# Decoder layer on one core: the Mamba time steps move into the samples' attention, and the first three stream units run in plain fp32

## The chip, the cores and the metric

One core of a Trainium2 chip runs the whole layer as one launch. The metric is the device time of that launch in microseconds (us), lower is better. The reference's inputs and outputs are fp32.

## What is computed

One decoder layer for a prompt of 1024 tokens and 8 samples of one token each, 1032 tokens in all, width 1024. Cut to what the change touches:

```python
mod = (silu(c) @ w_ada + b_ada)          # 9 rows (prompt, 8 samples), 6 parts: sh1 sc1 g1 sh2 sc2 g2
h = rmsnorm(x, norm1_g) * (1 + sc1) + sh1
z, xs, bm, cm, dtr, q, k, v, qi, ki, wi, gs, ga = split(h @ w_in)
dt = softplus(dtr + dt_bias); A = -exp(a_log)      # 32 heads
Acs = cumsum(dt * A)   # in each of 8 chunks of 128 tokens
decay_end = exp(Acs[-1] - Acs); chunk_decay = exp(Acs[-1]); exp(Acs)
y_attn = attend(q, k, v, qi, ki, wi)     # samples: pages of the cache, 64 of 257 keys kept
x = x + g1 * (merged @ w_out); h2 = rmsnorm(x, norm2_g) * (1 + sc2) + sh2; x = x + g2 * ffn(h2)
```

## The kernel before

The layer is a row of stages, each a block in which the five engines have instruction streams of their own, joined by semaphores; between two blocks all engines meet at a barrier. In order: `first_norm`, `project`, `select`, `attend` (prompt), `attend_samples`, `steps`, `stream`, `scan`, `merge`, `project_out_and_norm`, `ffn`. The token buffer `hT` holds h as 128 partitions x 8 x 1032, in fp32. A plain fp32 product is one matmul per 128 of the 1024 inputs, 8 for a unit of 128 outputs x 344 tokens. A split product writes each factor as a rounded half and a rest (`_hi`, `_lo`, fp32r) and takes three matmuls in place of one (`product`, L2253 to L2255), 24 for a unit.

**`attend_samples`** (L971). SP, ACT and POOL read the page table and issue page loads: SP first stores `qT` of the prompt (L1019, 4 MB), then 6 index-key pages and all 16 value pages; ACT 10 index-key pages; POOL all 16 key pages (L1008). TensorE (PE) turns the samples' small rows (L1034 to L1041), the index pages (L1048), makes the scores (L1056, L1059), turns the key pages (L1067), adds up mask and logits (L1071, L1075), turns the probabilities (L1080) and multiplies by the value pages (L1088). VectorE (DVE) finds the 64th score (L1144 to L1158), does the softmax (L1160 to L1166) and writes the result into `qT` (L1176); SP stores it (L1024), and the block ends when that has landed.

**`steps`** (L1180) stands between it and `stream`. SP loads a 0/1 table of heads, the modulation sums (`s_mod`, four partial sums over row groups) and its bias (L1209 to L1211). DVE makes dt by a chain of some 20 dependent instructions on 128 x 264 (L1302 to L1326), while ACT rounds `hT` (`s_h_hi`, L1228) and DVE then takes the rests (`s_h_lo`, L1330, written over `hT`). PE adds up the modulation (L1255), the decays (L1272 to L1274), spreads head values over partitions (L1279) and makes four gate tiles (L1263), which ACT copies and SP stores (L1217). POOL adds the bias (L1246) and splits the first two weight slabs for `stream` (L1352, L1354).

**`stream`** (L1361) makes the rest of the input projection in 102 units (34 blocks of 128 outputs x 3 token thirds), first 12 units of group 0's z, then for each further group 18 units of x/B/C and 12 of z. Unit u goes to PSUM bank u % 4 and waits until ACT has taken unit u-4 out of it (`keep_z` L1614, `keep_x` L1626). A weight slab of 256 outputs serves six units; POOL splits slab j+1 when unit 6j is free to overwrite the other half of `s_w_hi`/`s_w_lo`. Beside the units, DVE splits the cumulated decays (L1765, L1767) and makes the causal convolutions of group 0, six blocks f of five instructions each (L1679 a copy of the tail, L1680, three of L1683; `convolve`), then the samples' part; ACT's order is written out: the SiLU of block f (L1601) stands behind the copies of units 3, 4, 6, 8, 9 and 11 and waits for convolution f. After unit 11 PE turns the six tails (`raw_rows`, L1554, L1560), and after units 14 and 18 it spreads the samples' B and C, which POOL has laid out (L1507, L1571).

## Time and profile before

| | |
|---|---|
| median of 3 runs | 2978.61 us (2975.07 to 2980.99) |
| profiled execution, its own time | 2978.76 us |
| its span | 2977.0 us |
| PE busy | 2754.8 us, 93% of the span |
| DVE / ACT / POOL busy | 52% / 23% / 27% |
| mean clock granted to PE | 0.954 of full |

PE is the engine that bounds most of the span; the slices in which its digit falls below 9 are where another engine or a DMA decides. The granted clock has two levels, 1.2 and 2.4 GHz, 0.5 and 1.0 in the rows.

### The profile page before, as it was taken

The page shows a single profiled execution, that of the slowest core. Times are in us where ns is not written, and L with a number is a line of the kernel's source. Part 1 is how long each engine was busy: PE and PEld are TensorE (multiplying, and loading weights), DVE is VectorE, ACT ScalarE, POOL GpSimd, SP SyncE. Part 2 cuts the span into 40 slices and gives each one's busy share as a digit, 9 for nine tenths or more (in the row PEclk, how much of TensorE's full clock was granted, in tenths as well). Part 3 has the DMA queues.
Part 4 walks back from the last instruction along what each step waited for, and adds up shares of the span by engine and source line. Part 5 has one row for each costly group of instructions (what it writes and reads, how often), then busy time and mean ns, then how long its engine had stood idle before and what let it go on. Part 6 is the DMA issues. An engine that isn't in the chain of part 4 may idle for free. (4 is left out here: it accounts for less than half of the span.)

```text
span 2977.0 us, 40645 instructions
## 1 busy us (share of the span) xinstructions
PE 2754.8 (93%) x16375; PEld 2343.0 (79%) x16375; DVE 1546.4 (52%) x2733; ACT 680.7 (23%) x1432; POOL 812.0 (27%) x486
## 2 busy tenths in 40 slices
PE   7999999998996678999979979998979999999997
PEld 4888556666785368999956669998878989898986
DVE  3313399904553357665659963554634242525155
ACT  3121211105774211221247741101210000000001
POOL 0000430004321124434326642231242222232220
PEclk9999999997998679999989989999989999999999
DMA  6110234520002144434156644333111111111111
GB/s 219 46 58 22 68 121 151 170 71 11 2 2 101 54 138 145 136 107 143 58 141 197 184 139 140 114 100 107 29 44 49 51 43 43 43 43 45 55 29 57
DMA packets 288663, 258.63 MB, mean 87 GB/s; under 512 B 21273, under 2 KB 265361, under 8 KB 288290
## 3 DMA queue, kind: packets, MB, share of 16 engines
q1 hardware_dynamic: 254780, 190.35, 21.4%
q10 hardware_dynamic: 26176, 56.16, 5.2%
q0 software_dynamic: 7520, 9.51, 1.0%
q8 instruction: 131, 2.15, 0.3%
q14 instruction: 56, 0.46, 0.1%
HBM read 191.04 MB, written 65.06 MB: 86 GB/s over the span
## 5 line engine op out<-in xcount | busy, mean ns | idle before, releaser
L2253 PE MATMUL ps<-h_lo,w_hi 128*128 128x344 f32 x1504 | 482.5, 321 | 18.0 <-DVE h_lo L2372 11.1
L2254 PE MATMUL ps<-h_hi,w_hi 128*128 128x344 f32 x1504 | 481.4, 320 | 0.0
L2255 PE MATMUL ps<-h_hi,w_lo 128*128 128x344 f32 x1504 | 481.3, 320 | 0.0
L2235 POOL CAST w_hi<-ring 128x2048 fp32r<-128x2048 f32 (+1 forms) x50 | 96.4, 1928 | 813.5 <-PE ps L2255 785.5
L2253 PEld LDWEIGHTS ps<-h_lo,w_hi 128*128 128x128 f32 x1504 | 284.1, 189 | 19.1 <-issue 18.4
L2255 PEld LDWEIGHTS ps<-h_hi,w_lo 128*128 128x128 f32 x1504 | 283.9, 189 | 0.0
L2254 PEld LDWEIGHTS ps<-h_hi,w_hi 128*128 128x128 f32 x1504 | 283.6, 189 | 0.2
L2253 PE MATMUL ps<-s_h_lo,s_w_hi 128*128 128x344 f32 x816 | 265.4, 325 | 0.0
L2254 PE MATMUL ps<-s_h_hi,s_w_hi 128*128 128x344 f32 x816 | 260.8, 320 | 0.0
L2255 PE MATMUL ps<-s_h_hi,s_w_lo 128*128 128x344 f32 x816 | 260.8, 320 | 0.0
L467 PE MATMUL ps<-ring,hT 128*128 128x256 f32 (+3 forms) x1152 | 237.8, 369 | 5.9 <-PEq L119 5.9
L2691 DVE TENSOR_TENSOR ps<-ps,f_silu 128x344 f32<-128x344 f32 x66 | 34.6, 525 | 392.9 <-ACT f_silu L2657 392.9
L2237 POOL TENSOR_TENSOR w_lo<-ring,w_hi 128x2048 fp32r<-128x2048 f32 (+1 forms) x50 | 234.2, 4683 | 4.0
L467 PEld LDWEIGHTS ps<-ring,hT 128*128 128x128 f32 (+1 forms) x1152 | 197.2, 182 | 43.9 <-issue 8.7
L618 PE MATMUL ps<-hT,ring 128*128 128x344 f32 x768 | 227.2, 455 | 0.0
L618 PEld LDWEIGHTS ps<-hT,ring 128*128 128x128 f32 x768 | 144.3, 190 | 80.9 <-ACT sig L653 5.4
L2657 ACT ACTIVATE f_silu<-ps 128x344 f32<-128x344 f32 x66 | 30.3, 458 | 719.7 <-PE ps L2255 719.7
L681 DVE TENSOR_SCALAR_CACHE_REDUCE reached<-score,threshold_bits 128x384 uint8<-128x384 f32 (+5 forms) x192 | 171.5, 943 | 35.7 <-POOL score L574 33.4
L888 DVE CUSTOM_DVE_ANT_0 prob<-ps,sel_bias 128x128 f32<-128x128 f32 (+7 forms) x128 | 96.9, 757 | 155.7 <-PE ps L819 154.7
L2253 PE MATMUL ps<-w_lo,a_hi 128*128 128x512 f32 (+1 forms) x396 | 157.2, 397 | 8.5 <-DVE f_scaled L2704 8.4
L2253 PEld LDWEIGHTS ps<-s_h_lo,s_w_hi 128*128 128x128 f32 x816 | 153.7, 188 | 2.6 <-issue 2.6
L2255 PE MATMUL ps<-w_hi,a_lo 128*128 128x512 f32 (+1 forms) x396 | 155.8, 393 | 0.0
(415 smaller groups left out, 5229.6 us busy)
## 6 DMA issues: line engine op xcount, KB each, us to landing
ring<-in_w_ada SPq DMA_DIRECT2D x24, 1024.0 KB, 7.5
ring<-in_w_in SPq DMA_DIRECT2D x23, 1024.0 KB, 5.7
ring<-in_w_ffn_in SPq DMA_DIRECT2D x44, 512.0 KB, 4.8
ring<-in_w_in SPq DMA_DIRECT2D x24, 512.0 KB, 8.4
s_post<-post ACTq DMA_DIRECT2D x24, 512.0 KB, 2.6
post_chunk<-s_post SPq DMA_DIRECT2D x32, 384.0 KB, 3.7
ring<-in_w_ffn_out SPq DMA_DIRECT2D x10, 1024.0 KB, 5.1
s_sig<-sig ACTq DMA_DIRECT2D x16, 516.0 KB, 6.9
```

Source lines behind the costliest of these rows:

```text
L467: mm = nc.tensor.matmul(ps[0:r, (9 * s + t) % 4, 0:width], hT[:, k, P * t:P * t + r], w[:, k, 0:width], start=(k == 0), stop=(k == KB - 1))
L618: mm = nc.tensor.matmul(ps[:, j % 4, 0:CW], w[:, k, 0:P], hT[:, k, CW * c:CW * c + CW], start=(k == 0), stop=(k == KB - 1))
L681: a = v.tensor_scalar(reached[:, at:at + P * (i + 1)], score_of(i), thr_f[:, i:i + 1], None, ALU.is_ge, ALU.add, accum_out=count[:, i:i + 1])
L888: nc.vector.tensor_tensor_reduce(out=prob[:, n % 2, 0:L], in0=ps[:, 2 * (n % 2):2 * (n % 2) + 2, :].rearrange("p a n -> p (a n)")[:, chunk ...
L2235: self.nc.gpsimd.tensor_copy(hi, raw).then_inc(self.hi_done, 1)
L2237: self.nc.gpsimd.tensor_tensor(lo, raw, hi.bitcast(F32), ALU.subtract).then_inc(self.split, 1)
L2253: nc.tensor.matmul(out, ah, bl, start=(i == 0), stop=False)
L2254: nc.tensor.matmul(out, ah, bh, start=False, stop=False)
L2255: mm = nc.tensor.matmul(out, al, bh, start=False, stop=(i == len(terms) - 1))
L2657: nc.scalar.activation(silu[:, i % 2, :], ps[:, 2 * (i % 3), 0:CW], ACT.Silu).then_inc(silu_done, 1)
L2691: v.tensor_tensor(prod, prod, silu[:, i % 2, :], ALU.mult).then_inc(act_done, 1)
```

## The change

The block `steps` is gone. Its chain for dt, the decays, the modulation, the head spread and the gates are worked out inside `attend_samples`, in gaps of each engine's stream. The bias of the modulation is no longer added by POOL: it is loaded into rows 16 to 24 of the same tile, and a 0/1 matrix `pick` adds it up with the partial sums. The gates are kept as 9 rows and spread over 128 partitions when they are loaded later. Key and value pages share one buffer, so a value page is loaded when its sample's key pages have been turned. The loads are placed anew on the three queues. The rounding of `hT` and the taking of its rests move into `stream`, on ACT and DVE; the first three units (the first block, three token thirds) are made from `hT` and the unsplit slab in plain fp32, and a third's rest is written over `hT` when its plain unit is done. POOL splits slabs 0 and 1 inside `stream`. The diff, cut (the parts of `steps` that come back word for word in `attend_samples` stand there once):

```diff
@@ attend_samples @@
-def attend_samples(K, T):
+def attend_samples(K, T, S):
...
-        kpage, vpage = sb("kpage", [P, DEC, NPAGE, 256]), sb("vpage", [P, DEC, NPAGE, 256])
+        kpage = vpage = sb("kv_page", [P, DEC, NPAGE, 256])
...
         @block.gpsimd
         def _(pool):
             pool.wait_ge(table_in, 16)
-            load_pages(pool, "cache_k", kpage, k_in, 0, 16)
+            load_pages(pool, "cache_k", kpage, k_in, 0, 8)
 
         @block.sync
         def _(sp):
             sp.dma_start(pages[:], A["page_table"].rearrange("b j -> (b j)").unsqueeze(0)).then_inc(table_in, 16)
             sp.dma_start(who[:], A["k_who"]).then_inc(who_in, 16)
+            sp.wait_ge(table_in, 16)
+            load_pages(sp, "cache_kidx", ipage, i_in, 0, 8)
+            load_pages(sp, "cache_k", kpage, k2_in, 8, 16)
             sp.dma_start(A["s_att"].rearrange("k p n -> p k n")[:, :, 0:SEQ], T.qT[:, :, 0:SEQ]).then_inc(y_out, 16)
-            sp.wait_ge(table_in, 16)
-            load_pages(sp, "cache_kidx", ipage, i_in, 0, 6)
-            load_pages(sp, "cache_v", vpage, v_in, 0, 16)
+            for b in range(DEC):
+                sp.wait_ge(pe_key, b + 1)
+                load_pages(sp, "cache_v", vpage, v_in, NPAGE * b, NPAGE * b + NPAGE)
+            for i in range(2):
+                sp.wait_ge(gate_done, i + 1)
+                sp.dma_start(A["s_gates"][i], mod[0:9, 3 * D * i:3 * D * i + D]).then_inc(gate_out, 16)
             sp.wait_ge(y_done, 1)
             sp.dma_start(A["s_att"].rearrange("k p n -> p k n")[:, :, SEQ:NT], T.qT[:, :, SEQ:NT]).then_inc(y_out, 16)
             sp.wait_ge(y_out, 32)
+            sp.wait_ge(gate_out, 32)
...
-            pe.wait_ge(step, 1)
+            pe.wait_ge(step, 4)
...
-            pe.wait_ge(k_in, 16 * DEC * NPAGE)
+            pe.wait_ge(k_in, 16 * 8)
+            pe.wait_ge(k2_in, 16 * 8)
...
+            pe.wait_ge(dta_done, 1)
+            dta = S.dta[:].rearrange("p c h -> p (c h)")
+            mm(ps[:, 0, 0:NC], K.le[:], dta, start=True, stop=True)
+            mm(ps[:, 0, NC:2 * NC], K.gt[:], dta, start=True, stop=True)
+            mm(ps[:, 1, 0:NC], K.ones[:], dta, start=True, stop=True).then_inc(sums, 1)
+            pe.wait_ge(mod_in, 48)
+            pe.wait_ge(pick_done, 5)
+            for a, part in enumerate((1, 2)):
+                for k in range(KB):
+                    m = mm(ps[:, 2, (8 * a + k) * 9:(8 * a + k) * 9 + 9], mod[:, D * part + P * k:D * part + P * k + P], pick[:],
+                           start=True, stop=True)
+            m.then_inc(modT_ps, 1)
...
+            pe.wait_ge(sdec, 1)
+            pe.wait_ge(modT_step, 1)
+            pe.wait_ge(head_in, 16)
+            for b in range(INNER // P):
+                m = mm(ps[:, 2, 144 + 17 * b:144 + 17 * b + 17], mod[0:HEADS, D + P * b:D + P * b + P], spread[:],
+                       start=True, stop=True)
+            m.then_inc(spread_ps, 1)
...
+            pe.wait_ge(decays, 3)
+            for i, bank in enumerate((0, 4)):
+                for h in range(2):
+                    m = mm(ps[0:9, bank + h, :], pick[:], mod[:, 3 * D * i + 512 * h:3 * D * i + 512 * h + 512],
+                           start=True, stop=True)
+                m.then_inc(gate_ps, 1)
...
+            nc.scalar.activation(a_row[:], K.heads_row[:, 1, :], ACT.Exp).then_inc(a_done, 1)
+            nc.scalar.activation(a_col[:], K.heads_col[:, 1:2], ACT.Exp).then_inc(a_done, 1)
+            act.wait_ge(arg_ready, 1)
+            nc.scalar.activation(e[:], e[:], ACT.Exp).then_inc(dt_exp, 1)
             act.wait_ge(table_in, 16)
-            load_pages(act, "cache_kidx", ipage, i_in, 6, 16)
+            load_pages(act, "cache_kidx", ipage, i_in, 8, 16)
+            for rows in (slice(0, 16), slice(25, P)):
+                act.dma_start(mod[rows, :], A["s_mod"][rows, :]).then_inc(mod_in, 16)
+            act.dma_start(mod[16:25, :], A["b_ada"][0, 2 * D:6 * D].partition_broadcast(9)).then_inc(mod_in, 16)
...
+            act.wait_ge(modT_ps, 1)
+            act.dma_start(mod[0:HEADS, D:3 * D], A["k_head"]).then_inc(head_in, 16)
+            act.wait_ge(sdec_arg, 1)
+            nc.scalar.activation(spread[:, 0:DEC], spread[:, 0:DEC], ACT.Exp).then_inc(sdec, 1)
+            act.wait_ge(sums, 1)
+            for src, dst in ((ps[:, 0, 0:NC], S.e_acs), (ps[:, 0, NC:2 * NC], S.d_end), (ps[:, 1, 0:NC], S.c_dec)):
+                nc.scalar.activation(dst[:].rearrange("p c h -> p (c h)"), src, ACT.Exp).then_inc(decays, 1)
...
+            for i, bank in enumerate((0, 4)):
+                act.wait_ge(gate_ps, i + 1)
+                nc.scalar.copy(mod[0:9, 3 * D * i:3 * D * i + D], ps[0:9, bank:bank + 2, :].rearrange("p a n -> p (a n)"))\
+                    .then_inc(gate_done, 1)
...
+            link(v.memset(u[:, NC:W], 0.0))
+            link(v.tensor_tensor(u[:, 0:NC].rearrange("p (c h) -> p c h", h=HEADS), K.dt_raw[:],
+                                 K.heads_row[:, 0, :].unsqueeze(1).to_broadcast([P, TT, HEADS]), ALU.add))
+            link(v.tensor_scalar(u[0:HEADS, NC:W], K.dtT_raw[:], K.heads_col[:, 0:1], None, ALU.add))
+            v.scalar_tensor_tensor(e[:], u[:], -1.0, u[:], ALU.mult, ALU.min).then_inc(arg_ready, 1)
...
+            dve.wait_ge(dt_exp, 1)
+            link(v.tensor_scalar(t[:], e[:], 2.0, None, ALU.add))
...
+            v.tensor_scalar(spread[:, 0:DEC], u[0:HEADS, NC:W], a_col[:], None, ALU.mult).then_inc(sdec_arg, 1)
+            v.scalar_tensor_tensor(S.which[:], K.ident[:, 0:GH], -1.0, K.ident[:, GH:2 * GH], ALU.mult, ALU.subtract)
+            v.tensor_copy(pick[:], K.ident[:, 0:9]).then_inc(pick_done, 1)
+            for q, c0 in enumerate((16, 32, 64, 96)):
+                dve.wait_ge(pick_done, q + 1)
+                v.tensor_tensor(pick[:], pick[:], K.ident[:, c0:c0 + 9], ALU.add).then_inc(pick_done, 1)
...
+            dve.wait_ge(modT_ps, 1)
+            v.tensor_copy(K.modT[:, 2:4].rearrange("p a k s -> p (a k s)"), ps[:, 2, 0:144]).then_inc(modT_step, 1)
...
+            dve.wait_ge(spread_ps, 1)
+            v.tensor_copy(S.hx[:].rearrange("p b s -> p (b s)"), ps[:, 2, 144:144 + 17 * 16])
@@ steps @@
-def steps(K, S):
...
@@ stream @@
-def stream(K, S):
+def stream(K, hT, S):
+    PLAIN = TC
...
                             sp.wait_ge(K.sw_split, j + 1)
+                            if j == 0:
+                                sp.wait_ge(gemm, PLAIN)
...
             v.memset(pre[:, :, 0:CONV - 1], 0.0).then_inc(conv_zeroed, 1)
+            split_stream_slab(K, S, pool, 0)
...
-                if 2 <= j + 1 < NSLAB:
+                if j + 1 < NSLAB:
...
-                    pe.wait_ge(K.sw_split, i // 2 + 1)
+                    pe.wait_ge(*(ring_landed(K, first) if u < PLAIN else (K.sw_split, i // 2 + 1)))
+                elif u == PLAIN:
+                    pe.wait_ge(K.sw_split, 1)
+                if PLAIN <= u < 2 * PLAIN:
+                    pe.wait_ge(h_split, u - PLAIN + 1)
...
+                if u < PLAIN:
+                    for k in range(KB):
+                        a = mm(ps[:, u % 4, 0:CW], slab_of(K, first)[:, k, w], hT[:, k, cols], start=(k == 0), stop=(k == KB - 1))
+                    a.then_inc(gemm, 1)
+                    return
...
+            for c in range(TC):
+                cols = slice(CW * c, CW * c + CW)
+                a.copy(h_hi[:, :, cols], hT[:, :, cols]).then_inc(h_rounded, 1)
...
+            for c in range(TC):
+                cols = slice(CW * c, CW * c + CW)
+                dve.wait_ge(h_rounded, c + 1)
+                dve.wait_ge(gemm, c + 1)
+                v.tensor_tensor(h_lo[:, :, cols], hT[:, :, cols], h_hi[:, :, cols].bitcast(F32), ALU.subtract).then_inc(h_split, 1)
@@ project_out_and_norm @@
-                sp.dma_start(gate[0:r, b, :], A["s_gates"][b, 0:r, :]).then_inc(gate_in, 16)
+                sp.dma_start(gate[0:r, b, :], A["s_gates"][0, 0].partition_broadcast(P) if b == 0 else A["s_gates"][0, 1:9, :]).then_inc(gate_in, 16)
@@ program @@
-    A["s_gates"] = nc.dram_tensor("s_gates", (4, P, D), F32, kind="Internal").ap()
+    A["s_gates"] = nc.dram_tensor("s_gates", (2, 9, D), F32, kind="Internal").ap()
...
+        with ExitStack() as place:
+            h_lo = place.enter_context(nc.sbuf_tensor("s_h_lo", [P, KB, NT], F32R, side="right"))
```

How the written order moves: PE in the samples' attention, from the last key page on (names: `kpage`/`kv_page` cache pages, `sbias` the mask, `mod` the modulation sums, `spread` the head values). Before:

```order
L1067 MATMUL ps<-ident,kpage 128x128 x3
L1071 MATMUL ps<-sbias,who 128x257 [waits sbias_done,skT_done]
L1075 MATMUL ps<-skT,sqx 128x257 x16
L1080 MATMUL ps<-ident,sprob 128x128 [waits sdiag_done]
L1080 MATMUL ps<-ident,sprob 128x128
L1081 MATMUL ps<-sdiag,whoT 8x128
L1085 MATMUL ps<-snew,v 128x128 [waits value_pages_in,spT_done]
```

Now, with the changed kernel's line numbers:

```order
L1095 MATMUL ps<-s_dta,le 128x256 [waits dta_done]
L1096 MATMUL ps<-s_dta,gt 128x256
L1097 MATMUL ps<-s_dta,ones 128x256
L1102 MATMUL ps<-mod_pick,mod 128x9 [waits mod_pick_done,mod3_in]
L1102 MATMUL ps<-mod_pick,mod 128x9 x15
L1107 MATMUL ps<-sbias,who 128x257 [waits sbias_done,skT_done]
L1111 MATMUL ps<-skT,sqx 128x257 x16
L1118 MATMUL ps<-spread,mod 128x17 [waits head_in,modT3_step,sdecay_done]
L1118 MATMUL ps<-spread,mod 128x17 x15
L1123 MATMUL ps<-ident,sprob 128x128 [waits sdiag_done]
```

19 matmuls stand ahead of the mask's and 16 more behind the logits; four more (L1137, the gates) end PE's stream.

POOL at the start of the stream (names: `s_w_hi`/`s_w_lo` a slab's halves, `segw` a table for the scan). Before:

```order
L1490 MEMSET pre 128x4x3
L1491 CAST segw<-ones 128x4096
L1494 DMA s_acs<-acs_rows 32x2x1024 [waits n1turned]
```

Now:

```order
L1437 MEMSET pre 128x4x3
L1295 CAST s_w_hi<-ring 128x2048 [waits slab_landed0]
L1297 TENSOR_TENSOR s_w_lo<-ring,s_w_hi 128x2048 [waits stream_w_rounded]
L1439 CAST segw<-ones 128x4096
L1442 DMA s_acs<-acs_rows 32x2x1024 [waits n1high_moved]
L1446 DMA segw<-s_acs 8x4x1024 [waits n1low_moved,acs_stored]
L1446 DMA segw<-s_acs 8x4x1024
L1295 CAST s_w_hi<-ring 128x2048 [waits slab_landed1]
L1297 TENSOR_TENSOR s_w_lo<-ring,s_w_hi 128x2048 [waits stream_w_rounded]
```

Two slab splits now stand in this block, one ahead of the cast of `segw` and one behind its loads. On DVE, at the same place:

```order
L1725 CAST acs_rows<-ps 32x1024 [waits n1sample_step]
L1727 TENSOR_TENSOR acs_rows<-ps,acs_rows 32x1024 [waits n1high_moved]
L1732 TENSOR_TENSOR s_h_lo<-hT,s_h_hi 128x8x344 [waits modT_step,n1mean] x3
L1639 COPY tail<-pre 128x11 [waits mod_product,n1turned]
L1640 TENSOR_SCALAR post<-pre,vecs 128x1024
```

The three subtractions that make the rests stand ahead of all six convolutions of group 0; before, the first convolution followed the split of the decays. (Semaphores are lent again under the name of an earlier owner, as `n1mean` here.)

## Rows read from the trace of the kernel before

**Rows 1.** Busy time by stretch: the samples' attention, then `steps`.

```profile
core 0: us, PE busy (x) PEld busy (x) DVE busy (x) ACT busy (x) POOL busy (x), PEclk, DMA share, GB/s
944.00:1026.50 82.50, 49.95 (x203) 32.36 (x203) 17.87 (x61) 10.61 (x22) 8.70 (x17) 0.63 0.33 109
1026.50:1086.50 60.00, 28.23 (x86) 18.52 (x87) 40.37 (x37) 12.82 (x15) 22.36 (x8) 0.59 0.17 61
```

**Rows 2.** Timeline, samples' loads: start us, us, engine, line [idle before <-releaser].

```profile
946.34 15.23 ACTq L1008 DMA_DIRECT2D ipage<-in_cache_kidx  x10
...
957.00 17.51 SPq L1008 DMA_DIRECT2D vpage<-in_cache_v  x16
...
964.87 3.60 PE L1048 MATMUL ps<-ident,ipage 128*64 128x128 f32 x16 [17.22 <-DMA ipage<-in_cache_kidx]
```

**Rows 3.** DMA issues of 940 to 1100 us: KB each, us to landing.

```profile
s_att<-qT SPq DMA_DIRECT2D x1, 4096.0 KB, 15.4
```

**Rows 4.** Timeline, the two gaps of PE at the mask and the softmax.

```profile
993.21 1.19 PE L1071 MATMUL ps<-sbias,who 8*128 8x257 f32 x2 [4.77 <-DVE sbias L1158]
...
1006.55 0.44 PE L1080 MATMUL ps<-ident,sprob 128*128 128x128 f32 x2 [2.71 <-DVE sdiag L1166]
```

**Rows 5.** Groups by line in `steps`: busy us, mean ns | idle before.

```profile
L1330 DVE TENSOR_TENSOR s_h_lo<-hT,s_h_hi 128x2752 fp32r<-128x2752 f32 x3 | 8.9, 3005 | 0.0
...
L1255 PE MATMUL ps<-mod_who,mod 128*128 128x9 f32 x32 | 7.0, 363 | 19.3 <-POOL mod L1246 19.3
L1279 PE MATMUL ps<-spread,head_x 32*128 32x17 f32 x32 | 7.0, 370 | 7.0 <-DVE modT L1333 7.0
...
L1238 ACT COPY gate_sb<-ps 8x1024 f32<-8x1024 f32 x2 | 2.0, 1000 | 0.8 <-PE ps L1263 0.8
...
L1272 PE MATMUL ps<-s_dta,le 128*128 128x256 f32 x2 | 1.2, 712 | 2.9 <-DVE s_dta L1322 2.9
```

**Rows 6.** Timeline, the end of the samples' attention, and the gates in `steps`.

```profile
1022.40 1.47 DVE L1176 COPY qT<-ps 64x16 f32<-64x16 f32 x8 [14.45 <-PE ps L1088]
1023.90 0.38 SPq L1024 DMA_DIRECT2D s_att<-qT  x1
1026.48 0.35 SPq L1209 DMA_DIRECT2D head_x<-in_k_head  x1
...
1048.54 6.25 PE L1263 MATMUL ps<-mod,mod_who 128*128 128x512 f32 x8
```

**Rows 7.** Plain and split units: a group of the page, and where 12 split units start and end.

```profile
L618 PE MATMUL ps<-hT,ring 128*128 128x344 f32 x768 | 227.2, 455 | 0.0
...
1090.05 0.66 PE L2253 MATMUL ps<-s_h_lo,s_w_hi 128*128 128x344 f32 x1
...
1136.07 0.55 PE L1554 MATMUL ps<-ident,small_rows 24*128 24x24 f32 x6
```

**Rows 8.** Timeline of DVE and POOL in the stream: convolutions 0 and 3, slab split.

```profile
1092.54 0.15 DVE L1679 COPY tail<-pre 128x11 f32<-128x11 f32 x1
...
1093.45 3.93 DVE L1683 SCALAR_TENSOR_TENSOR post<-pre,vecs,post 128x1024 f32<-128x1024 f32 x3
...
1113.54 1.91 POOL L1352 CAST s_w_hi<-ring 128x2048 fp32r<-128x2048 f32 x1 [12.80 <-PE ps L2255]
...
1113.90 1.57 DVE L1679 COPY tail<-pre 128x11 f32<-128x11 f32 x1 [7.01 <-DMA s_post<-post]
...
1115.53 5.12 POOL L1354 TENSOR_TENSOR s_w_lo<-ring,s_w_hi 128x2048 fp32r<-128x2048 f32 x1
...
1116.22 8.17 DVE L1683 SCALAR_TENSOR_TENSOR post<-pre,vecs,post 128x1024 f32<-128x1024 f32 x3
```

**Rows 9.** PE's one long wait in the stream, and the stretch behind it (columns of rows 1).

```profile
1173.28 3.57 PE L1571 MATMUL ps<-bc_diag,ones 128*128 128x512 f32 x4 [7.76 <-POOL bc_diag L1507]
...
1173.00:1177.00 4.00, 3.72 (x6) 1.82 (x7) 0.00 (x0) 0.87 (x2) 4.00 (x5) 0.56 0.53 203
```

**Rows 10.** A stretch within the logits: us, PE busy, clock, DMA share, GB/s.

```profile
1000.00:1004.00 4.00, 3.84 (x18) 1.00 0.00 0
```

More of the change, by code:

```diff
@@ L753, in _ @@
             sp.dma_start(own_head[:], A["k_head"][0:AH, 0:D]).then_inc(head_in, 16)
+            for s in K.finished:
+                sp.sem_clear(s)
         @block.gpsimd
@@ L991, in attend_samples @@
         stat = sb("sstat", [P, 4])
+        NC = TT * HEADS
+        W = NC + DEC
+        u, e, z, t, poly = (sb("dt_" + n, [P, W]) for n in "uezts")
+        a_row, a_col = sb("a_row", [P, HEADS]), sb("a_col", [HEADS, 1])
+        spread = sb("spread", [HEADS, 17])
+        mod = sb("mod3", [P, 4 * D])
+        pick = sb("mod_pick", [P, 9])
+        pick_done = K.sem("mod_pick_done")
+        mod_in, modT_ps, modT_step = K.sem("mod3_in"), K.sem("modT3_in_psum"), K.sem("modT3_step")
+        gate_ps, gate_done, gate_out = K.sem("gate_in_psum"), K.sem("gate_done"), K.sem("gate_stored")
+        arg_ready, dt_exp, a_done = K.sem("dt_arg"), K.sem("dt_exp"), K.sem("a_exp")
+        dta_done, sums, decays = K.sem("dta_done"), K.sem("decay_sums"), K.sem("decays_done")
+        sdec_arg, sdec, spread_ps = K.sem("sdecay_arg"), K.sem("sdecay_done"), K.sem("spread_in_psum")
+        k2_in, head_in = K.sem("more_key_pages_in"), K.sem("head_in")
         table_in, who_in = K.sem("page_table_in"), K.sem("who_in")
@@ L1158, in _ @@
             v.tensor_scalar(sbias[:], swk[:], -OFF, None, ALU.mult).then_inc(biased, 1)
+            dve.wait_ge(modT_ps, 1)
+            v.tensor_copy(K.modT[:, 2:4].rearrange("p a k s -> p (a k s)"), ps[:, 2, 0:144]).then_inc(modT_step, 1)
+            dve.wait_ge(modT_step, 1)
+            sc = K.modT[:, 3, :, :]
+            v.tensor_scalar(sc, sc, 1.0, None, ALU.add).then_inc(modT_step, 1)
+            dve.wait_ge(modT_step, 2)
+            v.tensor_tensor(sc, sc, K.vecs[:, 128:136].unsqueeze(2).to_broadcast([P, KB, 9]), ALU.mult)
             dve.wait_ge(pe_logit, 1)
@@ L2796, in program, with kept_right @@
-            K.finished, K.lent = K.lent, []
             with ExitStack() as rec:
                 S = Chip()
-                S.dt, S.dta, S.d_end, S.e_acs, S.c_dec = (sb("s_" + n, [P, TT, HEADS], rec) for n in ("dt", "dta", "end", "e", "c"))
-                S.hx = sb("s_hx", [P, INNER // P, 17], rec)
-                S.which = sb("which_head", [P, GH], rec)
-                S.ysT = K.ysT
-                mid.close()
+                with ExitStack() as att:
+                    K.finished, K.lent = K.lent, []
+                    T = Chip()
+                    T.qT = sb("qT", [P, KB, NT], att)
+                    T.v = sb("v", [P, TT + 1, KVH * HD], att)
+                    T.wi = sb("wi", [P, TT + 1, IH], att)
+                    T.q_s, T.k_s = sb("q_s", [DEC, D], att), sb("k_s", [DEC, KVH * HD], att)
+                    T.qi_s, T.ki_s = sb("qi_s", [DEC, IH * HD], att), sb("ki_s", [DEC, HD], att)
+                    T.dt_raw, T.dtT_raw = K.dt_raw, K.dtT_raw
+                    with ExitStack() as keys:
+                        T.kT = sb("kT", [P, KVH, SEQ], keys)
+                        T.bias = keys.enter_context(nc.sbuf_tensor("sel_bias", [P, BIAS_AT[TT]], BF16))
+                        with ExitStack() as index:
+                            T.kiT, T.qiT = sb("kiT", [P, SEQ], index), sb("qiT", [P, 2, SEQ], index)
+                            with ExitStack() as rope:
+                                K.cos, K.sin = (sb(n, [P, TT + 1, HD], rope) for n in ("cos", "sin"))
+                                project(K, hT, T)
+                                release(K.finished)
+                            select(K, hT, T)
+                        K.finished, K.lent = K.lent, []
+                        attend(K, T)
+                        release(K.finished)
+                    def kept_right(name, shape):
+                        return rec.enter_context(nc.sbuf_tensor(name, shape, F32, side="right"))
+                    S.dt, S.dta, S.d_end, S.e_acs, S.c_dec = (kept_right("s_" + n, [P, TT, HEADS]) for n in ("dt", "dta", "end", "e", "c"))
+                    S.hx, S.which = kept_right("s_hx", [P, INNER // P, 17]), kept_right("which_head", [P, GH])
+                    S.ysT, S.h_lo = K.ysT, h_lo
+                    attend_samples(K, T, S)
@@ L2804, in program @@
+                K.finished, K.lent = K.lent, []
+                S.segw = rec.enter_context(nc.sbuf_tensor("segw", [P, GROUPS, TT, P], F32R))
                 with ExitStack() as parts:
-                    S.h_lo, S.h_hi = (parts.enter_context(nc.sbuf_tensor(n, [P, KB, NT], F32R, side="right")) for n in ("s_h_lo", "s_h_hi"))
+                    S.h_hi = parts.enter_context(nc.sbuf_tensor("s_h_hi", [P, KB, NT], F32R, side="right"))
                     S.w_hi, S.w_lo = (parts.enter_context(nc.sbuf_tensor(n, [P, 2, SLAB], F32R, side="right")) for n in ("s_w_hi", "s_w_lo"))
-                    steps(K, S)
@@ L2808, in program @@
-                    release(K.finished)
-                    S.segw = rec.enter_context(nc.sbuf_tensor("segw", [P, GROUPS, TT, P], F32R))
-                    K.finished, K.lent = K.lent, []
-                    stream(K, S)
+                    stream(K, hT, S)
                 release(K.finished)
                 K.finished, K.lent = K.lent, []
-                merged = mid.enter_context(nc.sbuf_tensor("merged", [P, KB, NT], F32, side="right"))
-                scan(K, S, W, merged)
+                scan(K, S, W, hT)
```

194 lines of the change are left out of this document (21 added, 173 removed).

## The prediction

> **What bounds the kernel now.** I read the page first: PE is busy for 93% of the span, so time is won only where PE idles or runs at the half clock. The busy time by stretch shows such a place [rows 1]: the samples' attention and `steps` together hold 142.5 us in which PE works 50.0 of 82.5 and 28.2 of 60.0 us, at a mean clock of 0.63 and 0.59. In `steps` no engine fills the time: DVE has 40.4 us, POOL 22.4, PE 28.2. PE's first matmul there waits 19.3 us for POOL's bias addition, which waited for a load, and its head spread 7.0 us for DVE [rows 5]. In the samples' attention the timeline shows PE's gaps: 17.2 us until the index pages are there [rows 2], 4.8 us for the mask and 2.7 us for the softmax, both from DVE [rows 4]. The stream behind is the opposite: 12 units follow each other from 1090.05 to 1136.07 us without a gap [rows 7].
>
> **The change, term by term,** against the profiled execution, which took 2978.76 us itself (span 2977.0; the median is 2978.61, so no correction is needed).
>
> *`steps` goes*: from its first instruction at 1026.48 us [rows 6] to the start of the stream at 1086.5 [rows 1]: **-60.0 us**, its barrier included.
>
> *Loads of the samples*: ACT issued 10 index pages in 15.2 us, 1.52 each, while the 4 MB store that SP had issued first was moving for 15.4 us; behind that store SP issued 16 value pages in 17.5 us, 1.09 each [rows 2, 3]. PE started 3.3 us after ACT's last issue (961.6 to 964.9). Now 8 pages each are issued on SP and ACT ahead of the store. At 1.09 each they end at 946.3 + 8.7 = 955.1, and PE starts at 958.4: **-6.5 us**. If the pace stays 1.52, it is -3.0. Key pages follow on SP (8 more, until some 964) and are turned only after the scores. The last keys were turned at 993.21 - 4.77 = 988.4 [rows 4], now at 982; even if all 16 value pages were issued only then, 17.5 us later makes 999.5, and they are needed behind the softmax, at 1006.55 + 3.4 = 1010 by the terms below. DVE's dt chain goes into its wait for the scores; it costs nothing while it is shorter than that wait. In `steps` those small instructions took long only beside POOL's additions, and POOL adds nothing here.
>
> *PE ahead of the mask*: three sums of some 1.1 to 1.2 us (one of their rows stands) and 32 passes in 7.0 us for the modulation [rows 5], 10.4 us, of which 4.8 fit in the gap [rows 4]: **+5.6 us**. All these durations come from half-clock stretches; at the full clock the work would be 5.2 us and the term +0.4.
>
> *Head spread behind the logits*: 7.0 us [rows 5] against a gap of 2.7 [rows 4]: **+4.3 us**, at the full clock +0.8.
>
> *Gates at the end*: eight passes as in L1263, 6.25 us; a copy by ACT of 1.0 [rows 5, 6]; an issue of 0.4; then the issue and landing of the last store as now, 1026.48 - 1023.90 = 2.6. With 0.2 for handovers that makes 10.5 us behind PE's value products, where it was 1026.48 - 1022.40 = 4.1 [rows 6]: **+6.4 us**, with the passes at the full clock +3.3.
>
> *Plain units*: 768 passes of L618 are 48 plain units in 227.2 us, 4.73 each; a split unit takes 46.02 / 12 = 3.84 [rows 7]. Three: **+2.7 us**.
>
> *DVE's late start*: counted from the stream's start. Before, convolution 0 began at +6.0 (1092.54). Now the third rest waits for plain unit 2, which ends at 4.1 + 14.2 = +18.3, and takes 3.0 [rows 5]: DVE begins at +21.3, 15 us later. And it meets POOL there. DVE's tail copy took 1.57 us in place of 0.15, ending with POOL's cast, and three of L1683 took 8.17 in place of 3.93 while POOL's subtraction ran [rows 8]: the two engines take turns, whole instruction by whole instruction. POOL splits slab 0 and casts `segw` until about +10, waits some 7 for its store, splits slab 1 from about +19 and slab 2 from +29.4, the end of unit 5. With turns taken in that order the first convolution ends at +39 in place of +10.7, the next ones follow at 4.8 us each, and the sixth tail is read at about +59. Who waits: ACT's SiLU of block 0 stands ahead of its copy of unit 4, whose bank unit 8 needs (due at +36.9, starts at +40.6: 3.7 us; then 1.0 at unit 9); `raw_rows` comes at +56.9 and waits 2.9 for the sixth tail; the first spread behind unit 14 waits 1.6, since the samples' convolution follows DVE's backlog. Together 9.2 us. PE's existing wait of 7.8 us for POOL [rows 9] gets 1.7 shorter by this, as POOL is less behind: **+7.5 us**. The bounds are 0 (DVE and POOL never meet) and 11.
>
> The Trainium skill, page "SBUF — State Buffer", section "Who interferes with whom", has the loser of the shared port pair wait for the whole instruction, as rows 8 show, but lets a DVE instruction with one SBUF input run free; by that the split of the decays would not queue behind POOL, and this term would be about 0.8 us less.
>
> *Hidden*: POOL's splits are due at +21.8 (slab 0) and +29.4 (slab 1) and end near +7 and +28; if slab 1 is later, unit 6 waits one for one. ACT's three roundings lie beside the plain units, and the first is asked for at +8. The later gate loads move the same bytes ahead of a stage that PE fills.
>
> Sum: -60.0 - 6.5 + 5.6 + 4.3 + 6.4 + 2.7 + 7.5 = -40.0 us: **2939 us**.
>
> **Rivals.**
>
> *A. The samples' part is cheaper* (the added passes at the full clock). For it: the logits ran at clock 1.0 from 1000 to 1004 us [rows 10], and PE now has work in its gaps. Against it: the mean is 0.63 there, and the same passes left it at a mean of 0.59 in `steps` [rows 1]. The four terms become -6.5 + 0.4 + 0.8 + 3.3 = -2.0 in place of +9.8: 2927 us.
>
> *B. DVE's lag costs PE nothing* (four banks and a SiLU order with slack). For it: DVE idled 7.0 us ahead of convolution 3 [rows 8], so there was slack. Against it: the lag is 15 us before POOL is counted. Only +2.7 is left in the stream: 2931 us.
>
> *C. The new waits cost PE its clock.* PE's wait of 7.8 us was followed by a stretch at 0.56, in which four matmuls took 3.57 us; at the full clock these would be 3.57 x 0.56 = 2.0, so 1.6 us lost and some more in the unit behind, about 2 [rows 9]. Three waits of 2.9, 3.7 and 1.6 us would add up to 6: 2945 us. Against it: they are shorter than that one. The Trainium skill, page "TensorE: Matmul & The Clock Gate", section "Part 1: The HAM clock gate", lets the array fall back to the half clock after idling, which speaks for this rival; that a short idle is enough no row here shows.
>
> *D. The modulation load is late.* 2 MB more go through ACT's queue beside 2 MB of keys and the 4 MB store. At the store's pace (4 MB in 15.4 us) [rows 3] all of it takes some 31 us from 946, thus until 977, and PE asks at about 985. Eight us are in reserve; if the queues serve the load last and it lands at 995, PE waits 10 us: 2949 us.
>
> *E. Slower than before.* If the half clock of rows 9 doesn't end with one wait but holds through the z units of group 0 and beyond, because PE meets DVE's backlog at each bank, every unit costs 3.8 us more. The gain of 40 is gone after 10.5 of the 102 units; with 12 it is 2985 us. Against it: the 12 units of rows 7 began after 10 us without dense work and still average 3.84 us, so the clock comes back once units follow each other. That `steps` is not really removed is excluded: its instructions are absent from the written order.
>
> **How the numbers follow.** Sum as worked out 0.45, A 0.17, B 0.15, C 0.10, D 0.08, E 0.02; 0.03 for something I don't see, half of it slower. The forecast is the likeliest case. The range reaches to A (2927) and to D (2949) with the bounds of the terms beyond (A with a free stream is 2919, the longer lag 2943): 2924 to 2951 leaves out less than 2 in 10. A measurement of this kernel can tell 0.2%, 6 us, from no change; no case but E comes near that: faster 0.96, same 0.01, slower 0.03.
>
> **What would show it.** Index pages turned at about 958 us; the block of the samples ending near 1036, 91 to 93 us after its start in place of 82; in the stream two waits of PE on ACT near units 8 and 9, one on DVE's tails behind unit 11; three plain units of 4.7 us. Wrong it would be if PE waited in the samples' part for the modulation or the head table, if unit 5 waited for the third rest, or if units 3 to 8 took more than 3.9 us each.

## The result, and the profile after

| | before | changed |
|---|---|---|
| median, 20 runs of each, alternating | 2978.39 us (2973.71 to 2982.04) | 2982.47 us (2977.51 to 2987.88) |
| profiled execution, its own time | 2978.76 us | 2977.51 us |
| its span | 2977.0 us | 2975.7 us |
| PE busy, mean clock | 93%, 0.954 | 92%, 0.956 |

The ratio of the times is 1.0015, with a 95% interval of 1.0009 to 1.0021: the changed kernel is slower by some 4 us, less than the 0.2% that the prediction had taken for no change. The prediction was 2939 us, 2924 to 2951. It was wrong by 43 us. The profiled execution of the changed kernel is the lowest of its 20, 5 us under their median, so its trace is read for where time lies, and the medians say how much.

Four stretches divide the span: up to the first load of the samples' attention, that block (with `steps` where it is there), `stream` up to the first row store behind its last group, and the rest.

| stretch, us | before | forecast | changed | difference |
|---|---|---|---|---|
| up to the samples' attention | 944.1 | 944.1 | 942.5 | -1.6 |
| samples' attention (+ `steps`) | 142.4 | 92.2 | 135.6 | -6.8 |
| `stream`, up to that store | 386.4 | 396.6 | 397.8 | +11.4 |
| the rest | 1504.1 | 1504.1 | 1499.8 | -4.3 |

The stream cost what was forecast. The block did not: 43 us of the expected 50 are missing there. Its windows, as in [rows 1] (in the second fence PE alone is counted):

```profile
core 0: us, PE busy (x) PEld busy (x) DVE busy (x) ACT busy (x) POOL busy (x), PEclk, DMA share, GB/s
942.50:1078.00 135.50, 70.89 (x281) 46.38 (x281) 29.14 (x96) 14.25 (x31) 4.40 (x8) 0.58 0.27 85
```

```profile
core 0: us, PE busy (x), PEclk, DMA share, GB/s
984.00:994.00 10.00, 10.00 (x23) 0.50 0.06 26
994.00:1004.00 10.00, 2.73 (x6) 0.50 0.06 26
```

PE has 70.9 us of work and 64.6 us of nothing. The second fence shows what it waits for: from 984 to 1004 us the DMA engines are busy for 0.06 of their time, which is one of 16, and move 26 GB/s. The DMA issues of the block give the load (KB each, us to landing):

```profile
s_att<-qT SPq DMA_DIRECT2D x1, 4096.0 KB, 72.7
...
mod<-s_mod ACTq DMA_DIRECT2D x1, 1648.0 KB
```

1648 KB are the 103 rows 25 to 127 of `s_mod`, 16 KB each. At 26 GB/s they take 65 us. The 4 MB store, 15.4 us in [rows 3], now lands after 72.7 us; the reading, which the sum of bytes under `e9` bears out, is that a part of it is dealt to that same engine. Three waits of PE follow, each behind something that landed or ended late (timeline of ACT's queue and of PE, changed kernel):

```profile
953.28 1.02 ACTq L1150 DMA_DIRECT2D mod<-s_mod  x2
954.34 24.01 ACTq L1151 DMA_DIRECT2D mod<-in_b_ada  x1
```

```profile
979.02 1.92 PE L1071 MATMUL ps<-ident,ipage 128*64 128x128 f32 x8 [22.02 <-ACT siT L1154]
...
1008.52 6.86 PE L1091 MATMUL ps<-ident,kv_page 128*128 128x128 f32 x32 [11.78 <-DMA kv_page<-in_cache_k]
1030.80 6.99 PE L1102 MATMUL ps<-mod_pick,mod 128*128 128x9 f32 x32 [14.12 <-DMA mod<-in_b_ada]
```

The issue of the next load on ACT's queue is held for 24.0 us behind the 103 rows, and with it ACT's copy of the first index pages: PE waits 22.0. Then a key page is late, 11.8, then the modulation, 14.1. Together 47.9 us. (The trace names the bias load; the runs below say which load it was.) Behind it the value pages' issue on SP's queue is slow too, 30.4 us for 16 in place of 17.5 in [rows 2]; the slowest of them took 5.37 us, the median 0.37.

The stream, beside [rows 7] and [rows 8]: three plain units, the third rest, POOL's second slab split, the first two convolutions.

```profile
1081.69 14.62 PE L1498 MATMUL ps<-hT,ring 128*128 128x344 f32 x48
```

```profile
1092.74 3.84 POOL L1295 CAST s_w_hi<-ring 128x2048 fp32r<-128x2048 f32 x1
1096.66 7.25 POOL L1297 TENSOR_TENSOR s_w_lo<-ring,s_w_hi 128x2048 fp32r<-128x2048 f32 x1
```

```profile
1096.43 3.03 DVE L1732 TENSOR_TENSOR s_h_lo<-hT,s_h_hi 128x2752 fp32r<-128x2752 f32 x1 [1.60 <-PE ps L1498]
1099.38 4.58 DVE L1639 COPY tail<-pre 128x11 f32<-128x11 f32 x1
...
1108.55 1.87 DVE L1639 COPY tail<-pre 128x11 f32<-128x11 f32 x1
```

The plain units take 4.87 us each (4.73 in the forecast). DVE's tail copy of 0.15 us takes 4.58 while POOL subtracts: the two take turns, as [rows 8] had shown.

### The profile page after: what moved, and what is told of

It is laid out like the page before. It is cut to its first block and busy times, and to the rows that moved or that the text cites. A ratio compares the mean times of both kernels' runs of the same rounds, so it can differ in the third digit from the quotient of the medians.

```text
span 2975.7 us, 40570 instructions
## 1 busy us (share of the span) xinstructions
PE 2746.6 (92%) x16343; PEld 2335.3 (78%) x16343; DVE 1533.6 (52%) x2734; ACT 678.6 (23%) x1430; POOL 805.6 (27%) x475
## 5 line engine op out<-in xcount | busy, mean ns | idle before, releaser
L2218 PE MATMUL ps<-s_h_lo,s_w_hi 128*128 128x344 f32 x792 | 258.9, 327 | 2.4 <-ACT z_block L1571 2.4
L2220 PE MATMUL ps<-s_h_hi,s_w_lo 128*128 128x344 f32 x792 | 253.5, 320 | 0.0
L2219 PE MATMUL ps<-s_h_hi,s_w_hi 128*128 128x344 f32 x792 | 253.4, 320 | 0.0
L2219 PE MATMUL ps<-w_hi,a_hi 128*128 128x512 f32 (+1 forms) x396 | 155.8, 393 | 0.0
```

What stands on the lines that cost most here:

```text
L2218: nc.tensor.matmul(out, ah, bl, start=(i == 0), stop=False)
L2219: nc.tensor.matmul(out, ah, bh, start=False, stop=False)
L2220: mm = nc.tensor.matmul(out, al, bh, start=False, stop=(i == len(terms) - 1))
```

## The experiments

Theory 1: the load of 103 rows runs on one of the 16 DMA engines, because 103 is a prime, and whatever shares that engine lands late with it. The rival is that too many bytes are asked for at once (the change adds 2 MB beside keys and store), or that the order on ACT's queue is at fault. All runs but `e3` and `e8` start from the changed kernel.

**e1: the same bytes in rows that divide.**

```diff
-            for rows in (slice(0, 16), slice(25, P)):
+            for rows in (slice(0, 16), slice(25, 32), slice(32, P)):
...
-            pe.wait_ge(mod_in, 48)
+            pe.wait_ge(mod_in, 64)
```

> The changed kernel with one edit: rows 25 to 127 of the modulation sums, loaded there by one DMA of 103 rows, are loaded by one of 7 rows (25 to 31) and one of 96 (32 to 127); the bytes are the same. Theory 1 (a DMA of 103 rows runs on one DMA engine only, and what is queued behind it there waits): the load lands by about 975 us in place of 1030, ACT's issue of the bias no longer holds its queue for 24 us, key and value pages land in 3 us, the samples' block ends 92 to 95 us after its start in place of 135.6, the median is 2939 us (2933 to 2948). Rival (8 MB in one burst are too much in whatever shape): the waits of 22.0, 14.1 and 11.8 us of PE stay, 2982 us.

Measured: **2929.05 us** (2927.64 to 2929.93, 5 runs), ratio 0.9833 [0.9819, 0.9846]. Its PE in the block, the places of the fence above:

```profile
954.53 3.65 PE L1071 MATMUL ps<-ident,ipage 128*64 128x128 f32 x16 [9.36 <-DMA ipage<-in_cache_kidx]
...
971.44 5.09 PE L1091 MATMUL ps<-ident,kv_page 128*128 128x128 f32 x24
...
977.71 0.60 PE L1095 MATMUL ps<-s_dta,le 128*128 128x256 f32 x2
...
979.00 3.63 PE L1102 MATMUL ps<-mod_pick,mod 128*128 128x9 f32 x32
982.57 1.17 PE L1107 MATMUL ps<-sbias,who 8*128 8x257 f32 x2
...
993.66 4.63 PE L1118 MATMUL ps<-spread,mod 32*128 32x17 f32 x32
998.22 0.69 PE L1123 MATMUL ps<-ident,sprob 128*128 128x128 f32 x2
...
1015.46 5.94 PE L1137 MATMUL ps<-mod,mod_pick 128*9 128x512 f32 x8
```

The time is 4 us under the range that I had expected (2933 to 2948). All three waits are gone with one more cut in a load; the block takes 84.3 us. The bytes and their order on the queue are those of the changed kernel, so the rival of too many bytes falls. Run again beside the later ones:

> The kernel of the run with rows 25 to 31 and 32 to 127 loaded apart, once more, as the base for the three runs beside it. It took 2929.05 us, 0.983 of the kernel before. Expected by every theory: 2927 to 2931 us, ratio 0.982 to 0.985.

Measured: 2929.11 us (2926.07 to 2930.95, 5 runs), ratio 0.9832 [0.9819, 0.9846]. The block took 88.0 us here, since the last index page landed later: PE turned the first 16.7 us after the block's start, 13.0 in the first run.

**e2: 102 rows.** The cut at 26 in place of 32: `(slice(0, 16), slice(25, 26), slice(26, P))`.

> As the 96-row kernel, but cut into 1 row (25) and 102 rows (26 to 127). Theory 1, with the number of DMA engines being the largest divisor of the rows up to 16: 102 rows use 6 engines, 17 rows of 16 KB each, at the 26 GB/s that one engine moved in the changed kernel some 11 us: within 6 us of the 96-row kernel, 2939 to 2948 us. Rival (any number of rows that is no multiple of 16 falls to one engine): as the changed kernel, 2975 to 2990 us.

Measured: 2931.28 us (2930.54 to 2932.02, 2 runs), ratio 0.984 [0.9822, 0.9858]. One row fewer than 103 gives back 51 us, and since this load starts at row 26, a start at row 32 is not what helps. PE waits 4.3 us for a key page, and the store lands after 24.4 us in place of 20.1 in `e1`.

**e3: the kernel before, with a load of 103 rows put in.**

```diff
-            sp.dma_start(mod[:], A["s_mod"]).then_inc(mod_in, 16)
+            for rows in (slice(0, 25), slice(25, P)):
+                sp.dma_start(mod[rows, :], A["s_mod"][rows, :]).then_inc(mod_in, 16)
...
-            pool.wait_ge(mod_in, 32)
+            pool.wait_ge(mod_in, 48)
```

> The kernel before with one edit: in the steps block the load of the modulation sums, one DMA of 128 rows, is cut into one of 25 and one of 103 rows. Theory 1: 103 rows of 16 KB on one DMA engine at 26 GB/s take 65 us from 1027 us, so POOL's bias addition starts at about 1092 in place of 1037 and all of PE's modulation work and the gates behind it: 50 to 60 us slower, 3030 to 3040 us. Rival (the cost lies in the crowd of loads in the samples' block, not in the shape): no change, 2978 us.

Measured: 3025.11 us (3024.27 to 3025.94, 2 runs), ratio 1.0155 [1.0137, 1.0174], 46 us more, where 50 to 60 were expected. POOL's bias addition, and a window ahead of it:

```profile
1097.64 9.09 POOL L1247 TENSOR_TENSOR mod<-mod,mod_bias 9x2048 f32<-9x2048 f32 x3 [64.25 <-DMA mod_bias<-in_b_ada]
```

```profile
1040.00:1080.00 40.00, 0.00 (x0) 0.50 0.06 27
```

So the cut does the same where nothing else of size is being moved: 0.06 of the DMA, 27 GB/s, for 40 us. No issue was held here behind the 103 rows (the bias load's took 0.46 us).

**e9: is it the hold of ACT's queue?** The changed kernel with the bias load issued ahead of the two of `s_mod`, 103 rows kept.

> The changed kernel with one edit: the load of the bias rows stands ahead of the two loads of the partial sums on ACT's queue, so that nothing is issued behind the 103 rows until PE has used them; the 103 rows stay one load. Theory 1 (the 103 rows run on one of 16 DMA engines, and their landing sets the end): ACT's issue is held for less than 2 us, the index pages' copies and the scores come some 20 us earlier (scores done near 972), but PE then waits 30 us or more in all for key pages and modulation, and the modulation still starts at 1017 to 1031: 2970 to 2983 us, at most 13 under the changed kernel. Theory 2 (what costs is that ACT's queue is held, and the load itself would be in time): 2950 us or less, with PE's modulation products before 1000.

Measured: 2985.11 us (2981.22 to 2989.22, 10 runs), ratio 1.0014 [1.0005, 1.0023]: the changed kernel's own ratio, and theory 1, though 2 us above its range.

```profile
952.46 0.62 ACTq L1149 DMA_DIRECT2D mod<-in_b_ada  x1
953.11 0.70 ACTq L1151 DMA_DIRECT2D mod<-s_mod  x2
```

```profile
PE ps L1091 <- DMA kv_page<-in_cache_k: 26.8, 1, 26.8
PE ps L1102 <- DMA mod<-s_mod: 21.4, 1, 21.4
```

ACT is held by nothing, PE starts its scores some 20 us earlier, and then waits 26.8 + 21.4 = 48.2 us in place of 47.9. The modulation starts at 1031.71 us, and at 1030.80 in the changed kernel. The 24 us at the queue were cover for a landing that would have been waited for anyway. It fits a sum of bytes: that engine has the 1648 KB, a sixteenth of the 4 MB store (256 KB), of the 2 MB of keys (128 KB) and of the 256 KB of `s_mod`'s first rows (16 KB), 2048 KB; at 26 GB/s that is 81 us from 953.1, thus 1034; the store landed at 962.75 + 73.0 = 1035.8.

**e11: two engines.** Rows `(slice(0, 16), slice(25, 34), slice(34, P))`: 94 rows, divisible by 2.

> The changed kernel with rows 25 to 127 loaded as 9 and 94 rows: 94 divides by 2 and by 47. Theory 1 (a load is dealt to the largest number of DMA engines up to 16 that divides its rows, each at the 26 GB/s seen for 103 rows): 94 rows of 16 KB run on 2 engines at some 52 GB/s, 1504 KB in 29 us, so they land near 985 to 993; PE waits 3 to 12 us for the modulation, the DMA share is 0.12 once the other loads are done, and the time is 2932 to 2942 us. Theory 2 (a load this near to 96 rows is as good as 96, and it was the odd count or the size of 103 that hurt): no wait, 2929 us. A miss of theory 1 by a longer wait (PE waits 20 us or more, over 2950 us) would say that engines shared with other queues count for more than the rate.

Measured: 2950.32 us (2947.09 to 2953.62, 4 runs), ratio 0.9901 [0.9886, 0.9916].

```profile
981.00:986.00 5.00, 0.00 (x0) 0.50 0.12 52
```

```profile
PE ps L1091 <- DMA kv_page<-in_cache_k: 19.2, 1, 19.2
```

Two engines of 16, 52 GB/s, as expected; the time was not. I had counted the 1504 KB alone and a wait at the modulation. PE waits at the key pages, because their share on the two engines queues behind those rows; with 752 + 256 + 128 + 16 = 1152 KB on each, 26 GB/s gives 45 us from 955.3, thus 1001; the keys were there at 995.8 and the store at 1006, 5 us to either side. The row series is 96, 102, 94, 103 rows: 2929, 2931, 2950 and 2982 us, with 0, 4.3, 19.2 and 47.9 us of PE's waits in this stretch behind the index pages.

The Trainium skill, page "DMA: Bandwidth & Descriptors", section "Why a DMA increments its semaphore by 16 and not by 1", states this rule: a copy runs on the largest number of engines up to 16 that divides the slowest dimension of both sides, and it gives 127 partitions as a case of one engine. The traces agree where they show a rate (one engine at 103 rows, two at 94); for 102 and 96 rows they show only that the lateness shrinks and goes. The prediction did not use the rule and should have: the diff has `slice(25, P)` in it.

**e8: the order of the loads alone,** in the kernel before:

```diff
-            sp.dma_start(A["s_att"]...[:, :, 0:SEQ], T.qT[:, :, 0:SEQ]).then_inc(y_out, 16)
             sp.wait_ge(table_in, 16)
-            load_pages(sp, "cache_kidx", ipage, i_in, 0, 6)
+            load_pages(sp, "cache_kidx", ipage, i_in, 0, 8)
+            sp.dma_start(A["s_att"]...[:, :, 0:SEQ], T.qT[:, :, 0:SEQ]).then_inc(y_out, 16)
```

> The kernel before with one part of the change alone: SP issues 8 index pages ahead of its 4 MB store, ACT the other 8. Theory 1 (my term of the loads): PE turns its first index page 13 to 14.5 us after the block's start in place of 20.9, and the kernel takes 5 to 8 us less, 2971 to 2974 us, ratio 0.9975 to 0.998. Theory 2 (what PE gains there it loses at the value pages, which now stand behind a store in full flow): a wait of PE for the value pages appears behind the softmax, and the time is within 3 us of the kernel before.

Measured: 2972.47 us (2968.33 to 2977.76, 6 runs), ratio 0.9969 [0.9957, 0.9981].

```profile
956.96 3.65 PE L1048 MATMUL ps<-ident,ipage 128*64 128x128 f32 x16 [8.78 <-DMA ipage<-in_cache_kidx]
```

The block starts at 944.08, so PE turns pages at +12.9 in place of +20.9 [rows 2], and there is no wait for value pages. The next block comes 6.1 us earlier; by the ratio the whole gains 9 us, with 6 inside its interval.

**e12: three queues for the index pages** (6 on SP, 5 on ACT, 5 on POOL), on top of `e1`.

> On top of the load in divisible pieces: the 16 index pages are issued on three queues (6 on SP, 5 on ACT, 5 on POOL ahead of its key pages) in place of two (8 and 8). Theory 1 (my term of the loads: the issue of the pages, 1.09 us each, sets when PE turns them): PE starts 2 to 3 us earlier, 10 to 11 us after the block's start in place of 13.0, keys are still there in time, and the time is 1 to 3 us less, 2926 to 2928 us. Theory 2 (the landing of the last pages, or POOL's slower issue of 1.15 us a page, sets it): no gain or a wait for key pages, 2929 us or more.

Measured: 2927.82 us (2920.97 to 2934.36, 5 runs), ratio 0.9827 [0.9809, 0.9845]: the same as `e1`. The last issue is over at 952.7 us, 8.1 after the block's start (11.0 in `e1`), and PE still starts at +14.4. The slowest page took 6.6 us to land (median 1.9). So the landing of the last page sets it, as theory 2 says, and it varies: with the pages on two queues PE's start was at +12.6 to +16.7 in ten traces. The time of 2927.8 us lies in theory 1's range, but can't be told from `e1`.

**e5, e7, e10: the parts of the stream,** each on top of `e1`. `e5` puts ACT's SiLUs later:

```diff
-            first_silu = [3, 4, 6, 8, 9, 11]
+            first_silu = [5, 6, 8, 9, 10, 11]
```

> On top of the load in divisible pieces: ACT's SiLUs of blocks 0 to 5 stand behind the copies of units 5, 6, 8, 9, 10 and 11 in place of 3, 4, 6, 8, 9 and 11. Theory 1 (my term of the late start: the SiLU of block 0 holds ACT's copy of unit 4, whose bank unit 8 needs): PE's wait of 2.4 us on ACT at unit 8 goes, PE's other waits stay, time 2926 to 2928 us, 1 to 3 us under the base. Theory 2 (the wait only moves to a later bank, since DVE's backlog is what is late): a wait of 1 to 3 us on ACT at units 10 to 13, and 2929 us again.

Measured: 2930.9 us (2929.87 to 2935.42, 5 runs), ratio 0.9843 [0.9829, 0.9856].

```profile
PE ps L1517 <- DVE tail L1639: 8.8, 1, 8.8
```

The wait at unit 8 is gone, as theory 1 says, and the one for the tails behind unit 11 grows from 2.0 to 8.8 us. PE only comes sooner to what is late. That is theory 2 in kind, with the wait at the tails and not at a bank, and longer than it had.

`e7` has no plain units (`PLAIN = 0`; unit c waits for the rest of third c, and DVE no longer for a plain unit).

> On top of the load in divisible pieces: no plain units. Unit c waits for the rest of third c, and DVE makes the rests as soon as ACT has rounded. PE starts its first unit after DVE's first rest and POOL's slab 0, about 7 us after the stream's start in place of 3.6: +3.5 us; three units become split, 3.84 in place of 4.9 each: -3.2 us; and DVE's convolutions start some 6 us earlier. Theory 1 (DVE's late start costs PE what the term says): the waits on ACT at unit 8 (2.4) and for the tails (2.0) vanish, 2924 to 2927 us. Theory 2 (the plain units are worth their place, since they cover roundings, rests and slab 0): PE waits 5 us or more ahead of its first three units for the rests, 2930 to 2934 us.

Measured: 2930.97 us (2924.01 to 2931.99, 5 runs), ratio 0.9838 [0.9824, 0.9852].

```profile
PE ps L2213 <- DVE s_h_lo L1727: 6.1, 1, 6.1
```

PE waits 6.1 us for the first rest, and its waits at unit 8 and for the tails are gone. The stream takes 398.7 us, with plain units 399.4 and 400.2 in the two traces of `e1` and 397.8 in the changed kernel's. So it came as theory 2 says, and what the plain units hide they cost again, within this spread.

`e10` moves POOL's split of slab 1 right behind slab 0, ahead of the cast of `segw`.

> On top of the load in divisible pieces: POOL splits slab 1 right behind slab 0, ahead of its cast for the scan's table and its loads, so that this split doesn't stand beside the first convolutions. Theory 1 (DVE and POOL take turns, my term of the late start): DVE's first tail copy takes 0.2 us in place of 4.6, convolution 0 ends about 26 us after the stream's start in place of 30.5, PE's wait of 2.4 us on ACT at unit 8 shrinks to 0 and that of 2.0 for the tails too: 2924 to 2927 us. Theory 2 (the lag comes from DVE's own work, and POOL's place is of no matter): convolution 0 takes as long as before, 2929 us.

Measured: 2929.71 us (2926.18 to 2932.72, 5 runs), ratio 0.9838 [0.9825, 0.9852].

```profile
1038.00 16.12 DVE L1732 TENSOR_TENSOR s_h_lo<-hT,s_h_hi 128x2752 fp32r<-128x2752 f32 x3 [3.03 <-PE ps L1498]
1054.04 0.16 DVE L1639 COPY tail<-pre 128x11 f32<-128x11 f32 x1
```

The tail copy takes 0.16 us, so the turns with POOL are real; but the cast that now stands there meets the rests, which take 16.1 us in all. Two of the three took 6.4 and 6.8 us, the other 3.0. Convolution 0 ends 30.0 us after the stream's start, 30.5 in `e1`; PE's wait at unit 8 shrinks from 2.4 to 1.1 us and that for the tails stays at 2.0. Neither theory holds whole: the turns cost what I said, and moving POOL's work moves them to other DVE instructions.

The best kernel of the study is the changed one with the load cut at row 32: 2929 us, 0.983 of the kernel before. None of the others on top of it can be told from it.

## Why the prediction was wrong, and where it was right

**The step that failed** is the price of the modulation load: the sum puts it at nothing and rival D at 10 us. Both go by one estimate: "At the store's pace (4 MB in 15.4 us) [rows 3] all of it takes some 31 us from 946, thus until 977 ... Eight us are in reserve". That took for granted that a load of 103 rows moves as the store of 128 does. It runs at 26 GB/s in place of 4 MB in 15.4 us (272 GB/s), and PE's modulation starts at 1030.8 us and not at 985. D had the kind of fault, a modulation load that is late, but gave another reason for it (the queues serve the load last), 10 us and a chance of 0.08; measured are 48 us of waits, of which 14 stand at the modulation itself and the others at ACT's queue and the key pages, which D had not. Such a wait had been named as what would show the forecast wrong ("if PE waited in the samples' part for the modulation"), and that is what the trace shows.

**The other terms** can be read in `e1`, where the load is in time (its trace against that of before; 50.3 us less in the span). Its 2929 us are 10 under the forecast; the table shows that several terms were off by some us, both ways, and the row of the rest of the span, which no term had, is more than half of the 10.

| term, us | forecast | measured in e1 |
|---|---|---|
| `steps` goes | -60.0 | -60.0 |
| loads of the samples, PE's first index page | -6.5 | -7.8 |
| PE ahead of the mask | +5.6 | -0.3 |
| head spread behind the logits | +4.3 | +2.3 |
| value products | 0 | +1.5 |
| gates at the end | +6.4 | +6.1 |
| plain units | +2.7 | +3.2 |
| DVE's late start: PE's waits | +7.5 | +6.8 |
| what is left of the stream's +13.8 | 0 | +3.8 |
| the rest of the span | 0 | -5.9 |

*Ahead of the mask and behind the logits* I took half-clock durations from `steps` [rows 5]. In `e1` the three sums and the modulation run at the full clock, 0.60 and 3.63 us where it was 1.2 and 7.0 (granted clock 1.00 from 977.7 to 982.6 us); the head spread takes 4.63 us in place of 7.0, at a mean clock of 0.79. PE goes from the last key page into the mask without an idle moment. That is rival A for these two terms, 7.9 us together; the gates stay mostly at the half clock (mean 0.61, 5.94 us for eight passes, 6.25 in [rows 6]), as the sum had it.

*The stream* is right in size, and in part by luck. In `e1` DVE begins 21.3 us after the stream's start, as worked out; the sixth tail is read at +57.3 (forecast +59). The first convolution ends earlier than forecast, at +30.5 and not +39: POOL's split of slab 1 was begun sooner (+15.8 for +19), and part of it fell on the rests. The second then meets POOL's split of slab 2 (three instructions of 8.14 us in place of 3.93) and ends at +41.2, so most of the backlog is there again. PE's waits, in `e1`:

```profile
PE ps L1528 <- POOL bc_diag L1455: 9.0, 2, 7.3
...
PE ps L2218 <- ACT z_block L1571: 2.4, 1, 2.4
PE ps L1517 <- DVE tail L1639: 2.0, 1, 2.0
PE ps L1534 <- DVE ysq L1713: 1.9, 1, 1.9
```

At unit 8 there are 2.4 us (forecast 3.7, and 1.0 more at unit 9), for the tails 2.0 (2.9), at the first spread 1.7 (1.6); POOL's long wait shrank from 7.8 to 7.3 (I had 1.7 less), and that for `ysq` grew by 1.2, which no term had. The 6.8 for 7.5 is a sum of such misses. So rival B, that the lag costs nothing, is wrong.

*Rival C* is wrong where it was stated: behind the waits at unit 8, for the tails and at the first spread the granted clock stayed at 1.00. But behind the wait of 1.9 us for `ysq`, 209 us after the stream's start, it fell to 0.50 for some 5 us, where the kernel before waited 0.7 us and kept it:

```profile
1229.80:1233.80 4.00, 3.30 (x21) 1.00 1.06 327
...
1237.80:1241.80 4.00, 4.00 (x15) 0.50 0.85 252
```

The idle time alone does not tell the two cases apart (2.4 us kept the clock, 1.9 us lost it), and no run here shows what does. PE's busy time in the stream grew by 6.9 us; the plain units are 3.2 of them. The split matmuls took 327, 321 and 321 ns in the mean in place of 325, 320 and 320, which over 2175 of them makes 3 us, and that stretch at the half clock is an estimated 2 to 3 of it. The stream's length itself varies: unchanged, it took 386.4 and 389.0 us in the traces of the kernel before and of `e8`.

*DVE beside POOL.* The forecast's aside was that the split of the decays might run free of POOL. It did, in 1.21 us each, as in the kernel before, in the midst of POOL's subtraction (1027.91 to 1032.47 us), while the tail copy waited for the next one:

```profile
1029.43 1.21 DVE L1725 CAST acs_rows<-ps 32x1024 fp32r<-32x1024 f32 x1 [12.40 <-PE ps L1538]
...
1047.07 4.57 DVE L1639 COPY tail<-pre 128x11 f32<-128x11 f32 x1
```

The copy, too, reads SBUF once, so the number of SBUF inputs, by which the aside went, does not decide it alone. The term does not change by it: DVE waited 3.0 us for the first plain unit behind the split.

*The rest of the span* is 5.9 us shorter in `e1` and in the changed kernel, though nothing was changed there that the waits show. The stretch from the stream's last group to the first gate load took 553.4 and 554.7 us in two traces of the kernel before (with `e8`), and 549.1 to 553.4 in ten traces of the changed kernel and its relatives. The two ranges touch, so this may be the spread between executions; whether some 2 us belong to the change stays open.

## What to carry to other kernels

Before a load is priced by its bytes, look at how many rows it has: one cut at a row number that leaves a prime cost 53 us here, nearly the 60 us of the stage that was removed. When a DMA's share in a window stands at 0.06 or 0.12 while everything waits, one or two engines carry the load, and every other transfer that is dealt over all engines is as late as its share there. And a wait that is removed in front of a later one on the same data, as ACT's queue in `e9` or the SiLU in `e5`, gives nothing: ask first what lands last.
